# Layer gates and values of a two-block transformer kernel: from 512-column groups in three products to 256-column groups with a joint moving operand

## The reference, cut to what matters

```
z = h @ w_in[l]                                   # 2048 x 4928
q_lat, kv_lat, k_rope, mla_gate, conv_in, conv_gate = split(z)
q  = (rms_norm(q_lat) @ w_q_up)   ;  kv = (rms_norm(kv_lat) @ w_kv_up)
attn    = causal attention over 8 heads of 128 + 64
mla_out = attn * silu(mla_gate)                   # mla_gate: 1024 columns
u_val, u_gate = split(conv_in + glu_b[l])         # 1024 columns each
u = u_val * sigmoid(u_gate)
u = depthwise causal convolution of u, 31 taps
u = silu(layer_norm(u)) @ w_pw + b_pw
y = concat(mla_out, u * silu(conv_gate)) @ w_out[l]
x = x + gate * y
```

## Time and profile before

| what | before |
|---|---|
| median of 3 runs | 1936.4 us (1936.32 to 1936.4) |
| the profiled execution | 1936.53 us, of it a span of 1934.7 us |
| TensorE matmuls busy | 1909.5 us, 99% |
| TensorE weight loads busy | 1668.7 us, 86% |
| VectorE busy | 1511.9 us, 78% |
| ScalarE busy | 1068.5 us, 55% |
| granted TensorE clock | full in each of the 40 slices |

### The profile page before, as it was taken

How to read it: one execution, slowest core, us unless ns; L and a number is a source line. 1 busy time by engine, 2 the same in 40 slices (tenths; PEclk the granted TensorE clock), 3 DMA queues, 4 the chain that set the end, 5 groups by cost and what they waited for, 6 DMA issues and landing times.

```text
span 1934.7 us, 27616 instructions
## 1 busy us (share of the span) xinstructions
PE 1909.5 (99%) x11390; PEld 1668.7 (86%) x11390; DVE 1511.9 (78%) x2094; ACT 1068.5 (55%) x1549; POOL 0.2 (0%) x4
## 2 busy tenths in 40 slices
PE   7999999999999999999999999999999999999999
PEld 6888888888888888888888889999888899998897
DVE  6577776868888777888888567999966669999764
ACT  5575766455655443555544475555664566366742
POOL 0000000000000000000000000000000000000000
PEclk9999999999999999999999999999999999999999
DMA  8443445947889999989999735544455455454553
GB/s 284 157 158 127 152 149 182 368 151 285 336 333 337 344 344 339 336 326 333 335 338 343 270 135 169 185 165 162 150 189 185 152 179 192 153 174 134 177 196 126
DMA packets 63981, 442.58 MB, mean 229 GB/s; under 512 B 7248, under 2 KB 7536, under 8 KB 12400
## 3 DMA queue, kind: packets, MB, share of 16 engines
q1 hardware_dynamic: 61920, 434.30, 63.0%
q10 hardware_dynamic: 1936, 6.51, 0.9%
HBM read 438.67 MB, written 2.11 MB: 228 GB/s over the span
## 4 chain that ended last, share of the span: by engine, by line
PE 90%; DVE 7%; ACT 2%; issue 1%; DMA 0%; ACTq 0%; DVEq 0%
PE PS L630 24%; PE PS L634 12%; PE PS L509 11%; PE PS L510 11%; PE PS L511 11%; PE PS L501 5%; PE PS L578 5%; PE PS L580 4%; PE PS L579 4%; DVE UG L1474 2%; DVE WL L1115 2%; ACT WH L1983 1%; PE PS L659 1%; DMA X<-in_x 0%; ACT S L2046 0%
## 5 line engine op out<-in xcount | busy, mean ns | idle before, releaser
L1983 ACT ACTIVATE WH<-RAW 128x1024 fp32r<-128x1024 f32 (+1 forms) x636 | 663.3, 1049 | 732.7 <-PE PS L634 260.4
L1115 DVE TENSOR_TENSOR WL<-RAW,WH 128x1024 fp32r<-128x1024 f32 (+1 forms) x636 | 765.8, 1208 | 361.4 <-ACT WH L1983 359.7
L630 PE MATMUL PS<-HT,WH 128*128 128x512 f32 x2040 | 646.9, 398 | 0.0
L634 PEld LDWEIGHTS PS<-HT,WL 128*128 128x128 f32 x2040 | 383.2, 188 | 90.5
L634 PE MATMUL PS<-HT,WL 128*128 128x256 f32 x2040 | 401.3, 278 | 0.0
L630 PEld LDWEIGHTS PS<-HT,WH 128*128 128x128 f32 x2040 | 311.0, 189 | 7.7 <-issue 7.2
L578 PE MATMUL PS<-HT,WH 128*128 128x256 f32 x880 | 254.0, 289 | 0.7 <-DVE HT L1166 0.4
L580 PE MATMUL PS<-HT,WL 128*128 128x256 f32 x880 | 249.4, 283 | 0.0
L579 PE MATMUL PS<-HT,WH 128*128 128x256 f32 x880 | 249.4, 283 | 0.0
L1124 DVE SCALAR_TENSOR_TENSOR RAW<-RAW,CB 128x2048 f32<-128x2048 f32 x96 | 219.2, 2284 | 0.0
L1474 DVE SCALAR_TENSOR_TENSOR UG<-UV,PK,UG 128x256 f32<-128x256 f32 x480 | 200.4, 477 | 0.0
(11 more groups left out here) (322 smaller groups left out, 1993.8 us busy)
## 6 DMA issues: line engine op xcount, KB each, us to landing
RAW<-in_w_in SPq DMA_DIRECT2D x112, 1024.0 KB, 4.8
RAW<-in_ada_w SPq DMA_DIRECT2D x96, 1024.0 KB, 6.7
RAW<-in_w_up SPq DMA_DIRECT2D x64, 1024.0 KB, 6.6
RAW<-in_w_down SPq DMA_DIRECT2D x64, 1024.0 KB, 6.3
RAW<-in_w_out SPq DMA_DIRECT2D x48, 1024.0 KB, 4.9
RAW<-in_w_pw SPq DMA_DIRECT2D x8, 1024.0 KB, 4.9
RAW<-in_w_in SPq DMA_DIRECT2D x8, 768.0 KB, 4.2
RAW<-in_w_q_up SPq DMA_DIRECT2D x6, 1024.0 KB, 4.8
```

Of the source, the lines that this page charges most:

```text
L630: e.matmul(bk[i][:, 0:512], wh[:, at], m["HT"][:, kt, :, :].rearrange("p a t -> p (a t)"), start=kt == 0, stop=False, skip_group_check=True)
L634: op = e.matmul(bk[i][:, 0:256], wl[:, at], HTh[:, kt, :], start=False, stop=kt == n.kts - 1, skip_group_check=True)
L1115: e.tensor_tensor(m[f"WL{j % NHL}"][:, 0:nk * w], m[f"RAW{i % NRAW}"][:, k0 * w:(k0 + nk) * w], m[f"WH{j % NHL}"][:, 0:nk * w].bitcast(F32 ...
L1983: e.activation(m[f"WH{j % NHL}"][:, 0:nk * w], m[f"RAW{i % NRAW}"][:, k0 * w:(k0 + nk) * w], ACT.Copy).then_inc(signals["high"], 1)
```

## The change

The second half of the convolution's gates, the second half of its values and the attention gates become 256-column groups and go through `joint_products`. The weights of these columns are packed accordingly. Around them:

- ScalarE copies a second part of each group (with the bias for the convolution's) where it took the sigmoid or the Silu from PSUM. VectorE adds the first part with `summed`, one half into the next group.
- The sigmoid of the second gates is one activation over four tiles, in the third of the four groups. The product of values and gates is `gated`, two tiles at a time, as in the first half; `glued` goes.
- The Silu of the attention gates is taken by `gates_done`, four tiles at a time, two halves into the second next group. `attend` waits for the signal `gates_on` instead of the group's own mark.

```
-GLU_VALUES, GLU_GATES, ... = ((0, 1), 6), (2, 7), (3, 4), 5, (8, 9), (10, 11, 12, 13)
-LAYER_JOINT = GLU_VALUES[0] + Q_LATENT + CONV_GATES
+GLU_VALUES, GLU_GATES, ... = \
+    ((0, 1), (6, 7)), (2, (8, 9)), (3, 4), 5, (10, 11, 12, 13), (14, 15, 16, 17)
+LAYER_JOINT = GLU_VALUES[0] + Q_LATENT + GLU_GATES[1] + GLU_VALUES[1] + MLA_GATES + CONV_GATES
...
-        "w_in2": (16, [256] * 2 + [512] + [256] * 2 + [384] + [512] * 4 + [256] * 4),
+        "w_in2": (16, [256] * 2 + [512] + [256] * 2 + [384] + [256] * 12),
...
 # TensorE
-        for g in (GLU_GATES[1], GLU_VALUES[1]):
-            products(group[f"w_in2_{L}", g], *hidden, h, cols=4)
+        for g in GLU_GATES[1] + GLU_VALUES[1]:
+            joint_products(group[f"w_in2_{L}", g], h)
...
-        for g in MLA_GATES:
-            products(group[f"w_in2_{L}", g], *hidden, h, cols=4)
-        for g in CONV_GATES:
+        for g in MLA_GATES + CONV_GATES:
             joint_products(group[f"w_in2_{L}", g], h)
...
 # VectorE
-                dve.wait_ge(*group[f"w_in2_{L}", MLA_GATES[h // 4]].taken)
+                dve.wait_ge("gates_on", 5 * L + h // 4 + 2)
...
-        course.group(group[f"w_in2_{L}", GLU_GATES[1]])
-        glued(GLU_VALUES[1], 4)
+        before = None
+        for k, g in enumerate(GLU_GATES[1] + GLU_VALUES[1]):
+            n = group[f"w_in2_{L}", g]
+            for j, _ in course.begin(n):
+                if k and j == n.first + 1:
+                    at = 4 + 2 * ((k - 1) % 2)
+                    summed(before, UG[:, at:at + 2, :] if k < 3 else UV[:, at:at + 2, 30:286])
+                if k == 3 and j == n.first + 2:
+                    gated(4)
+                if k == 3 and j == n.done - 1:
+                    summed(g, UV[:, 6:8, 30:286])
+                    gated(6)
+            before = g
...
-            before = next((g for g in CONV_GATES if group[f"w_in2_{L}", g] is n), None)
+                    at = 2 * (MLA_GATES + CONV_GATES).index(before)
+                    summed(before, MG[:, at:at + 2, :] if at < 8 else CG[:, at - 8:at - 6, :])
+            before = next((g for g in MLA_GATES + CONV_GATES if group[f"w_in2_{L}", g] is n), None)
...
 # ScalarE
-        conv_gate(GLU_GATES[1], 4)
-        course.group(group[f"w_in2_{L}", GLU_VALUES[1]])
+        for k, g in enumerate(GLU_GATES[1] + GLU_VALUES[1]):
+            n, at = group[f"w_in2_{L}", g], 4 + 2 * (k % 2)
+            for j, _ in course.begin(n):
+                if k == 2 and j == n.first + 2:
+                    act.wait_ge("joint_sum", 2 * joint_index(GLU_GATES[1][1], L) + 2)
+                    e.activation(UG[:, 4:8, :], UG[:, 4:8, :], ACT.Sigmoid).then_inc(signals["gates_on"], 1)
+                if k == 3 and j == n.done - 1:
+                    second_part(n, UV[:, 6:8, 30:286], ACT.Identity, glu[:, 6:8])
+            if k < 2:
+                second_part(n, UG[:, at:at + 2, :], ACT.Identity, glu[:, 8 + at:10 + at])
+            elif k == 2:
+                second_part(n, UV[:, 4:6, 30:286], ACT.Identity, glu[:, 4:6])
...
-        for k, g in enumerate(MLA_GATES):
-            n = group[f"w_in2_{L}", g]
-            course.group(n)
-            store_T(n, MG[:, 4 * k:4 * k + 4, :], ACT.Silu)
...
+            act.wait_ge("joint_sum", 2 * joint_index((MLA_GATES + CONV_GATES)[2 * half + 1], L) + 2)
+            part = (MG if half < 2 else CG)[:, 4 * (half % 2):4 * (half % 2) + 4, :]
+            e.activation(part, part, ACT.Silu).then_inc(signals["gates_on"], 1)
+
+        for k, g in enumerate(MLA_GATES + CONV_GATES):
             n = group[f"w_in2_{L}", g]
             for j, _ in course.begin(n):
-                if k == 2 and j == n.first + 2:
-                    gates_done(0)
-            second_part(n, CG[:, 2 * k:2 * k + 2, :])
+                if k in (2, 4, 6) and j == n.first + 2:
+                    gates_done(k // 2 - 1)
+            at = 2 * (k % 4)
+            second_part(n, (MG if k < 4 else CG)[:, at:at + 2, :])
```

More of the change, by code:

```diff
@@ L28 @@
 RECEIVES = sum(RECEIVE, ())
-GLU_VALUES, GLU_GATES, Q_LATENT, KV_LATENT, MLA_GATES, CONV_GATES = ((0, 1), 6), (2, 7), (3, 4), 5, (8, 9), (10, 11, 12, 13)
-LAYER_JOINT = GLU_VALUES[0] + Q_LATENT + CONV_GATES
+GLU_VALUES, GLU_GATES, Q_LATENT, KV_LATENT, MLA_GATES, CONV_GATES = \
+    ((0, 1), (6, 7)), (2, (8, 9)), (3, 4), 5, (10, 11, 12, 13), (14, 15, 16, 17)
+LAYER_JOINT = GLU_VALUES[0] + Q_LATENT + GLU_GATES[1] + GLU_VALUES[1] + MLA_GATES + CONV_GATES
 JOINT = tuple(g for g in MIX_ORDER if g != KEYS and g not in VALUES)
@@ L292, in weight_course @@
         weights(f"w_kv_up_{layer}", range(4))
-        weights(f"w_in2_{layer}", (GLU_GATES[1], GLU_VALUES[1]))
+        weights(f"w_in2_{layer}", GLU_GATES[1] + GLU_VALUES[1])
         weights(f"w_q_up_{layer}", range(3))
@@ L311, in weight_course @@
                 mark = ("joint_sum", 2 * joint_index(g, int(tensor[6])) + 2)
-            elif tensor[:4] == "w_pw" or tensor[:5] == "w_in2" and g == GLU_VALUES[1]:
+            elif tensor[:4] == "w_pw":
                 taken += 1
@@ L1849, in vector_program @@
         UV, UG = m["UV"], m["UG"]
-        CG = Y[:, 1, :].rearrange("p (h t) -> p h t", h=8)
+        MG, CG = (Y[:, i, :].rearrange("p (h t) -> p h t", h=8) for i in range(2))
         def summed(g, part):
@@ L1859, in gated @@
         def gated(c0):
-            dve.wait_ge(*group[f"w_in2_{L}", GLU_GATES[0]].taken)
-            dve.wait_ge("joint_sum", 2 * joint_index(c0 // 2, L) + 2)
-            tt("glu", UV[:, c0:c0 + 2, 30:286], UV[:, c0:c0 + 2, 30:286], UG[:, c0:c0 + 2, :], ALU.mult)
-        def glued(g, c0):
-            n = group[f"w_in2_{L}", g]
[L1867 to L1878, removed]
+            if c0 < 4:
+                dve.wait_ge(*group[f"w_in2_{L}", GLU_GATES[0]].taken)
+            else:
+                dve.wait_ge("gates_on", 5 * L + 1)
+            dve.wait_ge("joint_sum", 2 * joint_index(sum(GLU_VALUES, ())[c0 // 2], L) + 2)
+            tt("glu", UV[:, c0:c0 + 2, 30:286], UV[:, c0:c0 + 2, 30:286], UG[:, c0:c0 + 2, :], ALU.mult)
         course.pace = 1
@@ L1922, in vector_program @@
                 if before is not None and j == n.first + 1:
-                    at = 2 * CONV_GATES.index(before)
-                    summed(before, CG[:, at:at + 2, :])
-            before = next((g for g in CONV_GATES if group[f"w_in2_{L}", g] is n), None)
+                    at = 2 * (MLA_GATES + CONV_GATES).index(before)
+                    summed(before, MG[:, at:at + 2, :] if at < 8 else CG[:, at - 8:at - 6, :])
+            before = next((g for g in MLA_GATES + CONV_GATES if group[f"w_in2_{L}", g] is n), None)
         course.drain(side, norm)
@@ L1930, in vector_program @@
             dve.wait_ge("half_done", n.done)
-            dve.wait_ge("cg", 2 * L + 2)
+            dve.wait_ge("gates_on", 5 * L + 5)
             for f in range(4):
@@ L2198, in convolution @@
             for c in range(c0, c0 + 4) if turn_[0] == 0 else ():
[L2199 to L2202, removed]
+                act.wait_ge("glu", 4 * L + c // 2 + 1)
                 e.activation(UG[:, c, :], UV[:, c, 0:256], ACT.Identity, scale=dw[:, c, 0:1],
@@ L2718, in scalar_program @@
                 if cg == 0 and j == n.first + 2:
-                    gates_done(1)
+                    gates_done(3)
         course.drain(side, norm)
```

2 lines of the change are left out of this document (1 added, 1 removed).

## The result

The changed kernel takes 1939.01 us (median; 1938.85 to 1939.46) against 1936.45 us for the kernel before beside it: a ratio of 1.0013 with a 95% interval of 1.0007 to 1.0019. It is 2.6 us slower. The interval lies above 1, so it is a real loss, but within the 0.2% that was called no change. The forecast was 1939.3. The profiled execution has a span of 1937.3 us against 1934.7.

A forecast was written before the change was run, and what follows sets the result against it. TensorE and VectorE were both taken as full in the layer stretch. The terms gave +1.45 us a layer, +2.9 in all, on the profiled 1936.53: 1939.4, or 1939.3 as median; range 1935.3 to 1943.2.

The forecast's parts named there:

- Two engines that are both full: Layer stretch, 1252 to 1395 us: TensorE and VectorE arrive nearly together, neither with slack; VectorE busy 141.0 of 143.0 us.
- TensorE's saving, 0.093 us a half: Joint matmuls on TensorE: fewer weight loads save 0.093 us per eight-tile half, 3.0 us a layer, 5.9 in all.
- Step 1: Up to 1251.76 us, first layer: five converted halves bring TensorE and the start of VectorE's full stretch 0.46 us sooner.
- Step 2: 1251.76 to 1317.5 us: VectorE is the chain, +2.33, less a vanishing 0.38 us wait; with the earlier -0.46, +1.5 us.
- Step 3: 1317.5 to 1396.5 us: TensorE leads, 12 converted halves left, -1.1; alone it reaches the channel norm's sum at +0.4 us.
- Step 4: 1317.5 to 1396.5 us: attention-gate adds end VectorE's last taps +3.0 us later, cover 1.5, so TensorE passes at +1.45.
- Step 5: After the last taps: VectorE has air and nothing more changes; +1.45 us a layer, +2.9 in all.
- TensorE alone: Rival: TensorE alone sets the time, VectorE's adds falling into idle time; 1930.5 us, chance 0.10.
- Half and half: Rival: convolution half costs as forecast, but taps end inside the 1.5 us cover; +0.4 a layer, 1937.2 us, chance 0.20.
- ScalarE late: Rival: ScalarE, after VectorE's add and table loads, delivers weight halves late, cover 0.2 us; 1943.7 us, chance 0.20.

The follow-up runs named there:

- light taps: Every VectorE convolution tap cut from 256 to 128 columns, in both kernels: 1932.18 us for the kernel before, 1928.08 us for the changed kernel.
- the attention gates alone: Against the kernel before, only the attention gates go through the joint matmuls, the convolution half does not: 1936.14 us, ratio 0.9997.
- short adds: Changed kernel with VectorE's adds and gate products of the converted groups on 16 columns in place of 256: 1931.53 us, ratio 0.9974.
- the copies in place of the tables: Changed kernel with the sigmoid of the second gates and the Silu of the attention gates made plain copies: 1939.08 us, ratio 1.0013.

## Why the prediction was right, and where not

The total is right, and it is right by the forecast mechanism: VectorE's adds cost more than TensorE's loads save. Point by point:

- **What bounds it.** "Two engines that are both full" held. Shortening VectorE's adds moved the time by 7.5 us, shortening ScalarE's work by none.
- **TensorE's saving, 0.093 us a half.** Held where nothing lies between two halves, 2.79 for 2.88 us. Over all 32 of a layer it is 2.7 us and not 3.0. The Trainium skill's figures for one isolated gap ("TensorE: Matmul & The Clock Gate", Back-to-back issue gap), by which it would have been about a quarter of that, do not describe this stream.
- **Step 1, -0.46.** Right for VectorE (split at 1251.31 for 1251.76, -0.45). What it did not say is that the first add then stands ahead of the reciprocal HS in VectorE's queue, and TensorE comes sooner to the sum that needs it. VectorE's timeline after the change, to be held against the earlier trace rows:

```profile
1251.31 1.23 DVE L1114 TENSOR_TENSOR WL<-RAW,WH 128x1024 fp32r<-128x1024 f32 x1 [0.47 <-ACT WH L1981]
1252.45 0.75 DVE L1110 TENSOR_TENSOR UG<-PS,UG 128x256 f32<-128x256 f32 x2
1253.12 1.66 DVE L1473 SCALAR_TENSOR_TENSOR UG<-UV,PK,UG 128x256 f32<-128x256 f32 x4
1254.70 0.42 DVE L1110 TENSOR_TENSOR KV<-KV,SQR 128x256 f32<-128x256 f32 x1
1255.04 1.74 DVE L1535 RECIPROCAL HS<-HS 128x256 f32<-128x256 f32 x1
```

```profile
1256.93 1.15 PE L502 MATMUL PS<-HS,CN 32*128 32x256 f32 x16 [1.24 <-DVE HS L1535]
```

  VectorE comes to the reciprocal 0.22 us later (1255.04 for 1254.82), TensorE 0.6 us sooner, and the wait of 0.39 us is 1.24 now. TensorE's first half microsecond goes here, not at 1275. By the chain it did not move the total, since VectorE leads behind it anyway; no run tests this by itself. With light taps, where it does not lead, the same wait is 1.4 of the 1.8 us missing there.
- **Step 2, +1.5 at 1317.5.** Measured +1.46 on TensorE and +1.47 on VectorE at 1318. The wait of 0.38 us at 1293.44 is gone, as supposed, but two small errors cancel here: the wait was worth 0.48 us (VectorE's lateness falls from +1.95 to +1.47 over it), and VectorE's added work came to 2.4 us and not 2.33. The terms of 0.333 and 0.62 us are in the trace: from 1252.45 to 1253.12 two adds take 0.67, and a product of two tiles takes 0.60, from 1287.50 to 1288.10:

```profile
1287.50 0.68 DVE L1110 TENSOR_TENSOR UV<-UV,UG 128x512 f32<-128x512 f32 x1
1288.10 1.66 DVE L1473 SCALAR_TENSOR_TENSOR UG<-UV,PK,UG 128x256 f32<-128x256 f32 x4
```

- **Step 3, +0.4 of its own at 1396.5.** Measured +0.45 at the first output group, and 1397.70 - 0.71 - 1396.49 = +0.50 at the sum (1396.49 is its start in TensorE's timeline before; the 1396.56 of the earlier trace rows is the chain's).
- **Step 4, taps' end +3.0, TensorE +1.45.** The taps end at 1397.55, +2.6, and the sum waits 0.71 us where about 1 was forecast:

```profile
1395.90 1.65 DVE L1473 SCALAR_TENSOR_TENSOR UG<-UV,PK,UG 128x256 f32<-128x256 f32 x4
```

```profile
1397.70 1.07 PE L502 MATMUL PS<-UG,CN 128*32 128x256 f32 x16 [0.71 <-DVE UG L1473]
```

  This is the term that was off, by 0.4 us at the taps. The cover was off too, the other way: the sum starts 0.15 us after the last tap's end, so of the 1.52 us between 1394.97 and 1396.49 only 1.37 can be used. 2.58 - 1.37 = 1.21 is what TensorE loses, where 1.45 was forecast. With the attention gates alone it is off alike, +1.15 us at the last taps where 2.67 - 1.19 = 1.48 was counted, and there it can be followed split by split. VectorE's lateness goes +0.05, +0.71, +1.37, +2.03, a pair of adds at a time. The fourth pair coincides with the pause at 1369.64 and leaves +1.94, so that pause was worth 0.75 and not 0.66; the one at 1380.83 takes 0.62 and not 0.53, and 0.14 go in between. The pauses were 1.5 us and not the 1.19 of the brackets in the earlier trace rows.
- **Step 5, nothing behind it.** Held: +1.21 from there to the layer's end, and +2.46 behind the taps of the second layer.
- **The rivals.** TensorE alone: refuted by the time. It comes close only where VectorE is given air, in the runs with short adds and with light taps. Half and half: it needed taps that end inside the cover, and the sum waits for them in both layers. ScalarE late: refuted by the copies in place of the tables; its cover was given as 0.2 us, and 0.13 was left.

## What to carry to other kernels

A saving on the busiest engine is worth only what the engines that feed it can follow. Add up per beat what each engine does and compare it with the beat (here 2.72 us of 2.88 on VectorE); a form that moves work from TensorE to VectorE, here 0.093 us saved against 5.0 / 32 = 0.16 us added for each half, loses as soon as the beat is full. Before giving such a form up, look where the loaded engine is idle upstream: a dozen taps moved there turned the same attention gates from 0.4 us into 2.8 us. But compare with the best that such a move gives without the new form: then it is 1.2 us. And when work is put into an in-order queue, ask not only what it costs but for which instruction behind it another engine comes next: TensorE's first half microsecond went into one reciprocal behind one pair of adds.

## What was unexpected of the hardware

Half the columns did not make a tap half as long; the expectation had put the saving at 0.14 us of a tap, and it is 0.13. VectorE's timeline of the changed kernel with light taps:

```profile
1253.03 1.13 DVE L1473 SCALAR_TENSOR_TENSOR UG<-UV,PK,UG 128x128 f32<-128x128 f32 x4
1254.08 0.42 DVE L1110 TENSOR_TENSOR KV<-KV,SQR 128x256 f32<-128x256 f32 x1
```

Four taps of 128 columns take 1.05 us to the next start, 0.263 each; four of 256 take 1.58, 0.395 each. By these two lengths the step is 1.03 ns a column, and 0.13 us of a tap does not depend on its columns. The short adds show the same: two of 16 columns still take 0.16 us, where the two of 256 take 0.67.

```profile
1252.55 0.25 DVE L1110 TENSOR_TENSOR UG<-PS,UG 128x16 f32<-128x16 f32 x2
1252.71 1.67 DVE L1473 SCALAR_TENSOR_TENSOR UG<-UV,PK,UG 128x256 f32<-128x256 f32 x4
```

What had not been expected is that the idle time in brackets is less than a late engine can make good: 0.38, 0.66 and 0.53 us in brackets were worth 0.48, 0.75 and 0.62. The 0.09 us or so on each fits the rows, in which a split is 1.22 us long but the next instruction of a busy VectorE starts 1.14 us after it: a pause in brackets is counted from the longer of the two. Add that much to each bracket before calling a stretch full.
